# Two mixer layers on one Trainium2 core: where the index-score products stand among the gated unit's products

## The reference, cut to what matters

```python
p = h @ w_in[l]
u_val, u_gate, g_conv, c_q, c_kv, k_idx, w_idx, g_attn = jnp.split(p, offsets, axis=-1)
# conformer convolution: gated unit, then 31 causal taps over positions, then LayerNorm over channels
a = u_val * jax.nn.sigmoid(u_gate)                       # 512 channels
y = lax.conv_general_dilated(a, conv_w[:, None, :], ..., feature_group_count=D_CONV) + conv_b
# attention on 128 selected keys, chosen by an index score of 8 heads
s_raw = jnp.einsum("bthd,bsd->bths", qi_b, k_idx_f)      # 8 heads of depth 64
score = jnp.einsum("bth,bths->bts", w_b, jax.nn.relu(s_raw))
score = jnp.where(causal[None], score, -jnp.inf)
_, sel = lax.top_k(score, k_top)                         # k_top = 128
logits = jnp.einsum("bthc,btkc->bthk", q_b, kv_sel) * (KV_LORA ** -0.5)   # + bias, softmax, values
x = x + gate[:, None, :] * rmsnorm(y, g_post[l])
```

## Time and profile before

| | |
|---|---|
| median of 3 runs | 1760.4 us (1760.35 to 1762.58) |
| profiled execution, own time | 1762.22 us |
| its span in the trace | 1760.9 us |
| TensorE busy in the span | 1615.0 us (92%) |
| VectorE, ScalarE, GpSimd busy | 720.4, 480.1, 363.2 us |
| mean granted TensorE clock | 0.951 of full |
| first index score on VectorE, layer 0 and layer 1 | 1169.34 and 1488.23 us |

### The profile page before, as it was taken

The page is one execution under the profiler, slowest core; times in us unless marked ns, Lnnn a source line. Parts: engine busy times, 40 slices in busy tenths (PEclk is TensorE's granted clock), DMA queues, the critical chain, the costliest instruction groups (busy, mean ns, idle before and its releaser), DMA issues.

```text
span 1760.9 us, 15352 instructions
## 1 busy us (share of the span) xinstructions
PE 1615.0 (92%) x5808; PEld 791.8 (45%) x5808; DVE 720.4 (41%) x1525; ACT 480.1 (27%) x984; POOL 363.2 (21%) x348
## 2 busy tenths in 40 slices
PE   6998999999999799998888797999989999999998
PEld 3434446644554433333333333444455554445553
DVE  2856535254252321110110100549775143987612
ACT  2022242101122100000000001565365134735621
POOL 3800000001000112211111100148233012842500
PEclk9999999999999799998898988999999999999999
DMA  9511032457262799999999998601202130020101
GB/s 332 191 48 48 1 120 96 144 191 251 72 255 121 285 414 406 407 402 411 407 400 398 411 411 349 241 1 69 75 1 90 49 113 0 20 100 25 48 0 48
DMA packets 72977, 328.08 MB, mean 186 GB/s; under 512 B 10522, under 2 KB 13746, under 8 KB 60480
## 3 DMA queue, kind: packets, MB, share of 16 engines
q1 hardware_dynamic: 64976, 310.23, 45.4%
q0 software_dynamic: 6144, 10.52, 1.8%
q10 hardware_dynamic: 1776, 6.27, 0.9%
HBM read 320.60 MB, written 14.78 MB: 190 GB/s over the span
## 4 chain that ended last, share of the span: by engine, by line
PE 71%; DMA 20%; DVE 5%; ACT 2%; issue 1%; POOL 0%; SPq 0%; POOLq 0%; DVEq 0%; ACTq 0%
PE bank L190 68%; DMA arena<-in_w 16%; DMA arena<-h_rows,arena 3%; PE bank L2190 1%; DMA arena<-in_w_in 1%; DVE arena L2650 1%; ACT arena L2365 1%; DVE arena L2637 0%; DVE arena L2652 0%; PE bank L932 0%; PE bank L2137 0%; PE bank L683 0%; DMA y_rows<-arena 0%; PE bank L584 0%; DVE bank L2628 0%
## 5 line engine op out<-in xcount | busy, mean ns | idle before, releaser
L190 PE MATMUL bank<-arena 128*128 128x512 f32 (+10 forms) x4944 | 1513.4, 549 | 87.0 <-DMA arena<-in_w 51.1
L190 PEld LDWEIGHTS bank<-arena 128*128 128x128 f32 (+5 forms) x4944 | 689.3, 177 | 844.2 <-issue 785.3
L2812 POOL TENSOR_TENSOR arena<-arena 128x512 f32<-128x512 f32 x180 | 199.2, 1107 | 204.1 <-ACT arena L2418 186.2
L1834 DVE TENSOR_TENSOR arena<-arena,bank 64x512 f32<-64x512 f32 x32 | 22.1, 691 | 315.3 <-ACT arena L1254 315.3
L1890 POOL TENSOR_TENSOR arena<-arena 128x1 f32<-128x1 f32 (+2 forms) x44 | 34.2, 777 | 566.2 <-DVE arena L1288 339.8
L2418 ACT ACTIVATE arena<-arena 128x512 f32<-128x512 f32 x180 | 126.8, 722 | 20.8 <-POOL arena L2812 20.6
L1016 ACT COPY arena<-bank 128x512 f32<-128x512 f32 (+3 forms) x115 | 61.2, 538 | 231.3 <-PE bank L190 130.4
L1254 ACT ACTIVATE arena<-bank 64x512 f32<-64x512 f32 x32 | 18.9, 592 | 370.0 <-PE bank L190 370.0
L1911 POOL DMA_INDIRECT y_rows<-arena x32 | 32.2, 1008 | 413.4 <-PE bank L932 259.5
L1300 DVE SCALAR_TENSOR_TENSOR arena<-arena 128x512 f32<-128x512 f32 x84 | 78.4, 933 | 2.7
L1827 DVE TENSOR_TENSOR arena<-bank,arena 128x512 f32<-128x512 f32 x32 | 22.1, 692 | 110.9 <-PE bank L932 110.9
(11 more groups left out here) (267 smaller groups left out, 900.1 us busy)
## 6 DMA issues: line engine op xcount, KB each, us to landing
arena<-in_w SPq DMA_DIRECT2D x96, 2048.0 KB, 40.3
arena<-in_w_in SPq DMA_DIRECT2D x15, 2048.0 KB, 9.3
arena<-in_w_ada SPq DMA_DIRECT2D x12, 2048.0 KB, 9.9
arena<-in_w_out SPq DMA_DIRECT2D x6, 2048.0 KB, 7.7
arena<-in_w_xk SPq DMA_DIRECT2D x2, 2048.0 KB, 9.5
arena<-in_w_xv SPq DMA_DIRECT2D x2, 2048.0 KB, 12.3
arena<-in_w_xq SPq DMA_DIRECT2D x2, 2048.0 KB, 11.3
arena<-in_w_xo SPq DMA_DIRECT2D x2, 2048.0 KB, 10.0
```

The lines of the kernel that those rows point to most:

```text
L190: i = pe.e.matmul(o, l, r, start=first and j == 0, stop=last and j == len(pairs) - 1)
L2812: pool.e.tensor_tensor(yc, yc, k.prod[l][n % 4], ALU.add).then_inc(*k.pool.step("sum", l, f, j))
```

## The change

The 24 index-score products are no longer made in one stretch. TensorE makes them in five groups of 5, 5, 5, 5 and 4, with the gated unit's products u1, g1, u2 and g2 between the groups, and u3 and g3 behind the last. ScalarE takes the first two sigmoids inside its list of Relus (after n = 9 and n = 19) and the third after tap 28. VectorE adds up n = 0 to 9, does three rounds of best keys, multiplies quarter 1, adds up n = 10 to 14, does two rounds, and so on. The index scores get five banks in turn, 0, 1, 2, 3 and 6, and the gated unit other banks. No operation is added or removed, and no transfer is moved.

```diff
-U_BANKS = ((4,), (4,), (5,), (4,))
-G_BANKS = ((5,), (6,), (7,), (6,))
+U_BANKS = ((4,), (4,), (4,), (6,))
+G_BANKS = ((5,), (7,), (7,), (7,))
+IS_BANKS = (0, 1, 2, 3, 6)
...
-def pe_index_scores(k, pe, l, t):
+def pe_index_scores(k, pe, l, t, heads):
     nk = (t + 1) * 128
-    for h in range(8):
+    for h in heads:
...
-        b = k.banks.take(pe, k.act, "is", l, t, h, among=(2, 3, 0, 1, 6, 7))
+        b = k.banks.take(pe, k.act, "is", l, t, h, among=IS_BANKS)
...
-    for t in (3, 2, 1):
-        pe_index_scores(k, pe, l, t)
+    pe_index_scores(k, pe, l, 3, range(5))
+    pe_glu(k, pe, l, 1, "u")
+    pe_index_scores(k, pe, l, 3, range(5, 8))
+    pe_index_scores(k, pe, l, 2, range(2))
+    pe_glu(k, pe, l, 1, "g")
+    pe_index_scores(k, pe, l, 2, range(2, 7))
+    pe_glu(k, pe, l, 2, "u")
+    pe_index_scores(k, pe, l, 2, range(7, 8))
+    pe_index_scores(k, pe, l, 1, range(4))
+    pe_glu(k, pe, l, 2, "g")
+    pe_index_scores(k, pe, l, 1, range(4, 8))
     B.lend(SUM_BANK, V, "is", l, 23)
-    for f in (1, 2, 3):
-        pe_glu(k, pe, l, f, "u")
-        pe_glu(k, pe, l, f, "g")
+    pe_glu(k, pe, l, 3, "u")
+    pe_glu(k, pe, l, 3, "g")
...
-SIGMOID_AFTER = {27: 1, 38: 2, 48: 3}
+SIGMOID_AFTER = {28: 3}
 GATE_AFTER = {53: 0, 58: 1, 61: 2}
...
         if n % 2:
             act_tap(k, act, l, 4 + n // 2)
+        if n in (9, 19):
+            act_glu(k, act, l, 1 + n // 19)
...
-    for t in (3, 2, 1):
-        dve_index_scores(k, dve, l, t)
-    dve_best_keys(k, dve, l, 3, range(9))
+    dve_index_scores(k, dve, l, 0, 10)
+    dve_best_keys(k, dve, l, 3, range(3))
     dve_glu(k, dve, l, 1)
-    dve_best_keys(k, dve, l, 3, range(9, 16))
-    dve_best_keys(k, dve, l, 2, range(2))
+    dve_index_scores(k, dve, l, 10, 15)
+    dve_best_keys(k, dve, l, 3, range(3, 5))
+    dve_index_scores(k, dve, l, 15, 20)
+    dve_best_keys(k, dve, l, 3, range(5, 8))
     dve_glu(k, dve, l, 2)
-    dve_best_keys(k, dve, l, 2, range(2, 12))
+    dve_index_scores(k, dve, l, 20, 24)
+    dve_best_keys(k, dve, l, 3, range(8, 14))
     dve_glu(k, dve, l, 3)
-    dve_best_keys(k, dve, l, 2, range(12, 16))
+    dve_best_keys(k, dve, l, 3, range(14, 16))
+    dve_best_keys(k, dve, l, 2)
     dve_best_keys(k, dve, l, 1)
```

More of the change, by code:

```diff
@@ L2578, in dve_taps, with dve_index_scores @@
                 *V.step("tap", l, f, j))
-def dve_index_scores(k, dve, l, t):
+def dve_index_scores(k, dve, l, lo, hi):
     V = k.dve
[L2583 to L2586, removed]
+    for n in range(lo, hi):
+        t, h = 3 - n // 8, n % 8
+        nk = (t + 1) * 128
+        S = k.banks.views[SUM_BANK][:, 0:nk]
         r, w = k.tmp[R_TILES[n % 4]][:, 0:nk], k.WI[:, t, h:h + 1]
         dve.wait_ge(*k.act.done("is", l, t, h))
+        if n:
+            dve.wait_ge(*V.done("is", l, n - 1))
         if h == 0:
-            if n:
-                dve.wait_ge(*V.done("is", l, n - 1))
             dve.e.tensor_scalar(S, r, w, None, ALU.mult).then_inc(*V.step("is", l, n))
         else:
-            dve.wait_ge(*V.done("is", l, n - 1))
             dve.e.scalar_tensor_tensor(out=S if h < 7 else k.MADD[:, t, 0:nk], in0=r, scalar=w, in1=S, op0=ALU.mult,
```

## The result

The changed kernel takes 1770.6 us (median of 8 runs, 1767.03 to 1774.53), the kernel before 1760.7 beside it: ratio 1.0055 [1.0044, 1.0066], **9.9 us slower**. The forecast was 7.0 slower, and 1770.6 lies inside the range of 1762.5 to 1772.0. The direction and the place were right. The engine that ends last was not the one forecast: it was nearly a tie, and went to the rival (TensorE slowed by its clock, put at 0.25) by about 1 us in each layer.

The account below looks back on a forecast made before the run. It took TensorE as the chain for 102.5 us, then VectorE from the fourth bias add; VectorE's lateness of 3.4 + 2.5 plus 2 x 0.5 for GpSimd gave 6.9, say +7: 1767.4 us, range 1762.5 to 1772.0.

Parts of the forecast that it names:

- the rival: TensorE, at half clock behind its query wait, overtakes VectorE: 3.1 to 4.8 us a layer, 1767 to 1770; chance 0.25.
- VectorE late by 10.25 us: Layer 1, end of VectorE's taps: 11.0 us of new idle time less 0.75 for an earlier start.
- the reserves of 6.86 and 7.81: VectorE's waits for TensorE up to the fourth bias add, us in layers 1 and 0, taken off its lateness.
- The layer 0 term of 2.5: VectorE's net lateness in layer 0: 11.0 less 0.66 of small waits less 7.81, 2.5 us.
- That sigmoid is not set by TensorE (1536.8) but by GpSimd: Third sigmoid, layer 1: GpSimd's late sums hold it to 1538.2, leaving VectorE idle 3.85 us.
- The 8 us wait: TensorE, after four query products, waits some 8 us for a bank ahead of the fifth.
- the floor: Query products end 1.4 us late in each layer even without a clock change; deciding alone 1763.2 us, chance with cancelling 0.12.
- the forecast's engine: VectorE, whose lateness decides at the attention's fourth bias add: 1765 to 1769.5 us, chance 0.50.
- The attention is a relay ... and shifts as a whole: Behind the fourth bias add VectorE and TensorE alternate, so lateness there passes on with no further term.
- GpSimd contention, 0.5 a layer: VectorE's masks and best-key thresholds now beside a busy GpSimd cost 0.5 us more in each layer.
- 0 to 2.3: Range in us for each layer of the GpSimd cost: none, up to 0.39 on each of six VectorE instructions.
- the rare faster case: TensorE's 7 us pass through in each layer, 1746.4 us, or about 1753 for half; chance of faster 0.08.

Follow-up runs that it names:

- Experiment 3: The changed kernel with 28 instead of 12 of ScalarE's taps among the waiting Relus and the third sigmoid behind tap 41: 1771.8 us, ratio 1.0061.
- Experiment 2: The changed kernel with eight unused products on TensorE in its wait ahead of the fifth query product: 1773.9 us, ratio 1.0065.
- experiment 7: The changed kernel with groups of 8, 5, 5 and 6 heads, ScalarE's list as in the change: 1764.7 us, ratio 1.0025.
- experiment 8: The changed kernel with groups of 8, 5, 5 and 6 heads and ScalarE's taps moved into its gaps: 1750.4 us, ratio 0.994.
- experiment 1: The changed kernel with ScalarE's gates at taps 34 to 50 and query copies behind taps 51 to 58: 1775.8 us, ratio 1.0083.
- experiment 4: The kernel before, with 15 unused maxima on VectorE in each layer ahead of its own taps: 1770.9 us, ratio 1.0056.
- experiments 5 and 6: Experiment 3's kernel with five unused TensorE products ahead of the attention's first transposes, then also four ahead of the second: 1770.6 us, then 1764.7 us.

## Why the prediction was right, and where it was off

**VectorE late by 10.25 us: right in kind, small by 1 to 2.** In layer 1 it comes to its first bias add 108.28 us from the last "qi" copy; before, its taps ended and left it free at 1582.57 - 1485.74 = 96.83. That is 11.45 late; in layer 0, 12.5. Less the reserves of 6.86 and 7.81, VectorE alone gives 4.6 and 4.7 us, where the forecast had 3.4 and 2.5, plus 0.5 each for GpSimd. The new waits are 12.75 us in all, where the forecast summed 11.0. Part of the difference is TensorE's switch from products over 128 partitions back to products over 64, which the forecast priced at nothing. The weight loads of the changed kernel, layer 1:

```profile
1495.97 0.19 PEld L190 LDWEIGHTS bank<-arena 128*128 128x128 f32 x1 [0.24 <-issue]
1496.92 0.30 PEld L190 LDWEIGHTS bank<-arena 64*128 64x128 f32 x4 [0.76 <-issue]
```

The next load comes 0.95 us after the last one instead of 0.43, with nothing to wait for, ahead of each of the four groups that follow a gated product; out of a group the step is 0.52 to 0.94. The half microsecond is about the size of what the waits of 5.62 and 2.13 us have over the forecast's 4.9 and 1.65. The layer 0 term of 2.5 was the worst: it took 0.66 off for small waits, and VectorE was 1 us later there than in layer 1, for the reason given under GpSimd below.

**"That sigmoid is not set by TensorE (1536.8) but by GpSimd": wrong.** The wait was sized well (3.85, measured 4.05), its cause was not. Experiment 3 took GpSimd's chain out of it and 0.9 us went. There the sigmoid starts 52.6 us from the copy, released by TensorE; the forecast's 1536.8 makes it 51.3 with the handover. TensorE's third quarter thus ends some 1.4 us later than computed, and the switches above are in that.

**The 8 us wait: right; the floor: in kind.** TensorE waits 8.02 us, and resumes 95.1 us from the "qi" copy; the forecast's times put it at 93.7, so the floor of 1.4 us is 2.8 even at the full clock. GpSimd's last 47 sums run without a break and end at 1585.0, just clear of VectorE's 13 taps, which take 10.21 us as in the earlier trace rows.

**Which engine decides: the rival.** The last query copy is 5.66 us late: 1.4 is the forecast's floor, 1.4 the later resumption, and 2.9 the half clock (the last copy starts 9.98 us after the resumption, where four steps of 1.72 and the handover of 0.2 make about 7.1). The rival was to decide if the low spell cost over 2.0; it cost 2.9. So TensorE is 5.7 late where VectorE alone would be 4.6, and the difference is the 1.07 us that VectorE still waits; in layer 0 it is 0.69. The Trainium skill ("TensorE: Matmul & The Clock Gate", Why this matters for your kernels) has it that such a gap brings the half clock; the 0.50 from 1578 on agrees. Without the 2.9 the floor would be under VectorE's 4.6, and the forecast's engine would have decided. Experiment 2 shows that this tie-break is worth about 1 us a layer at the fourth bias add, and not in the total.

**"The attention is a relay ... and shifts as a whole": right for this kernel, by luck.** The stretch takes 73.6 us before and after. In these runs it stays so only where TensorE comes to the attention no earlier than VectorE, or neither is late (the change, experiments 7 and 8). In experiments 1, 3 and 4 TensorE is early and waits for VectorE, 8.06, 5.15 and 4.09 us in layer 1, and the stretch grows by 1 to 2.2 us. The filled waits of experiments 5 and 6 show the clock to be the cause. Had the forecast's own engine decided, TensorE would have been some 2 us early; the nearest run to that is experiment 2, where the stretch grew by 1.2 us in each layer, and the forecast had no term for it. So the total of 7 us fell near the 9.9 through a mechanism that was given 0.25. VectorE was later than forecast, which made the loss larger, and the clock loss in the attention, which the forecast left out, stayed away because TensorE was late too.

**GpSimd contention, 0.5 a layer: right in layer 0, of the wrong sign in layer 1.** From VectorE's first score to the end of its 13 taps, less its waits, it takes 93.6 / 94.3 us before and 94.1 / 93.9 in the change: 0.5 more, 0.4 less. This is the microsecond by which layer 0 was later. Most of what parts the two layers lies in the three causal masks, which are 128x128 in every case and take from 0.28 to 1.20 us beside GpSimd's sums, 1.74 / 2.70 us together before and 2.39 / 2.24 in the change. The last mask of layers 0 and 1, kernel before, then in the change:

```profile
1236.44 0.28 DVE L2606 TENSOR_TENSOR arena<-arena 128x128 f32<-128x128 f32 x1
1554.54 1.20 DVE L2606 TENSOR_TENSOR arena<-arena 128x128 f32<-128x128 f32 x1
...
1244.31 0.28 DVE L2616 TENSOR_TENSOR arena<-arena 128x128 f32<-128x128 f32 x1
1567.65 0.28 DVE L2616 TENSOR_TENSOR arena<-arena 128x128 f32<-128x128 f32 x1
```

The forecast's "0 to 2.3" counted such instructions as clear of GpSimd before, and they were not. Where VectorE's 13 taps themselves lie beside GpSimd the price is larger: 4.3 us in experiment 7. The Trainium skill ("GPSIMD Engine Reference", Specifications) speaks of shared SBUF interfaces for VectorE instructions with two SBUF inputs; 14.47 against 10.21 us agrees.

**Left open.** What makes the switch of 0.5 us; what sets whether a mask beside GpSimd takes 0.28 or 1.20 us; what sets the length of the low spell behind the LayerNorm. The forecast of the rare faster case asked for a VectorE and a GpSimd chain less late at once; experiment 8 is that case, and needed both.

## What to carry to other kernels

When work is dealt out between another engine's long products, count for each engine that follows how long its own work lasts until the next group arrives, and give it what fills that time; in program order, a waiting instruction starves everything behind it, here taps whose sums were needed 50 us later. Write down the reserve of every engine up to where they meet: with one mended, the next one's lateness shows, and only both together made it faster than before (0.994, against 1.0025 and 1.0061). In these runs a wait of 3 to 8 us on TensorE ahead of the attention had a second price through its clock, so that a delay on another engine cost 1 to 2 us more than it lasted.

## What the runs showed of the hardware

- TensorE's wait ahead of the attention's first transposes in layer 1, and the spell at a granted clock of 0.50 (1.2 GHz of 2.4) that began in it or just behind it: 3.07 us and about 3 us (experiment 2), 4.09 and 7 (experiment 4), 5.15 and 14 (experiment 3), 8.06 and 14 (experiment 1). In the last three, four transposes took 1.08 to 1.12 us instead of 0.60 to 0.66. A wait of 1.54 us there, in the changed kernel, was followed by no fall.
- Filling one such wait moved the drop to the next wait; filling both removed it, and took the stretch from 75.6 / 75.8 back to 73.6 us.
- From a 128-partition to a 64-partition product the next weight load came 0.95 us after the last, not 0.43.
- Thirteen taps of VectorE (128x512, float32) took 10.21 us with GpSimd idle and 14.47 with it busy. A 128x128 mask on VectorE took from 0.28 to 1.20 us beside GpSimd's sums.
